# First norm's sums between the first modulation blocks, and tables loaded behind the fourth

## The reference

```python
sh1, sc1, g1, sh2, sc2, g2 = jnp.split(jax.nn.silu(cond) @ p['ada_w'] + p['ada_b'], 6, axis=-1)
hn = rmsnorm(h, p['norm1']) * (1.0 + sc1) + sh1
m, ctx_out = mixer(hn, p['mix'], ctx)
...
def rmsnorm(x, g, eps=NORM_EPS):
    y = xf * lax.rsqrt(jnp.mean(xf * xf, axis=-1, keepdims=True) + eps)
```

## Time and profile before

| | |
|---|---|
| median of 3 runs | 2384.64 us (2384.18 to 2547.99) |
| profiled execution | 2387.17 us |
| its span | 2385.4 us |
| instructions | 41564 |
| TensorE, VectorE, ScalarE, GpSimd busy | 91%, 44%, 27%, 6% |
| mean granted clock of TensorE | 0.935 |

### The profile page before, as it was taken

How to read it: one execution, slowest core, us unless ns; L and a number is a source line. 1 busy time by engine, 2 the same in 40 slices (tenths; PEclk the granted TensorE clock), 3 DMA queues, 4 the chain that set the end, 5 groups by cost and what they waited for, 6 DMA issues and landing times.

```text
span 2385.4 us, 41564 instructions
## 1 busy us (share of the span) xinstructions
PE 2173.5 (91%) x18628; PEld 1811.6 (76%) x18628; DVE 1055.8 (44%) x1875; ACT 653.8 (27%) x1155; POOL 152.8 (6%) x145
## 2 busy tenths in 40 slices
PE   5998787889899999998999868999979899999997
PEld 3554334345799999998999447888855699999997
DVE  0104443331555555324354546867752455555412
ACT  1211332331333233212223433232211233233311
POOL 1000000000000000000000533122100000000000
PEclk8998776899999999998999969999989899999998
DMA  8011442261122221222221000000021122222122
GB/s 306 25 60 57 141 141 71 106 237 45 36 71 77 92 80 49 73 73 65 72 71 45 18 8 3 3 3 4 4 76 36 36 71 71 71 84 71 51 71 69
DMA packets 141409, 163.74 MB, mean 69 GB/s; under 512 B 2368, under 2 KB 106864, under 8 KB 141232
## 3 DMA queue, kind: packets, MB, share of 16 engines
q1 hardware_dynamic: 137872, 148.81, 19.4%
q0 software_dynamic: 3360, 12.28, 1.5%
HBM read 157.32 MB, written 3.75 MB: 68 GB/s over the span
## 4 chain that ended last, share of the span: by engine, by line
PE 82%; DVE 12%; ACT 2%; DMA 1%; issue 1%; ACTq 0%; POOL 0%; DVEq 0%; SPq 0%; POOLq 0%
PE ps L218 76%; PE ps L314 3%; DVE small L907 2%; DMA ring<-in_ada_w 1%; PE ps L829 1%; DVE work L371 1%; ACT work L1322 1%; DVE x_lo_r L384 1%; DVE work L920 1%; DVE work L1797 1%; PE ps L326 1%; DVE work L1361 0%; DVE work L919 0%; DVE stat L322 0%; PE ps L1525 0%
## 5 line engine op out<-in xcount | busy, mean ns | idle before, releaser
L218 PE MATMUL ps<-x_hi_r,w_lo 128*128 128x320 f32 x2080 | 475.9, 310 | 0.0
L218 PE MATMUL ps<-work 64*64 64x64 f32 (+6 forms) x4942 | 384.2, 276 | 36.3 <-DVE work L1862 7.4
L218 PE MATMUL ps<-x_hi_r,w_hi 128*128 128x320 f32 x1664 | 382.0, 311 | 11.3 <-DVE x_lo_r L384 11.3
L218 PE MATMUL ps<-x_lo_r,w_hi 128*128 128x320 f32 x1664 | 382.4, 311 | 8.2 <-DVE g_lo L551 8.2
L218 PEld LDWEIGHTS ps<-work 64*64 64x64 f32 (+4 forms) x4942 | 245.4, 150 | 161.0 <-issue 110.7
L218 PEld LDWEIGHTS ps<-x_hi_r,w_lo 128*128 128x128 f32 x2080 | 348.5, 188 | 0.9
L218 PEld LDWEIGHTS ps<-x_hi_r,w_hi 128*128 128x128 f32 x1664 | 278.9, 188 | 14.8 <-issue 8.6
L218 PEld LDWEIGHTS ps<-x_lo_r,w_hi 128*128 128x128 f32 x1664 | 280.7, 190 | 8.8 <-DVE g_lo L551 8.8
L427 DVE SCALAR_TENSOR_TENSOR work<-ps,par,work 128x511 f32<-128x511 f32 (+1 forms) x188 | 103.5, 550 | 284.2 <-ACT work L527 276.6
L474 DVE TENSOR_TENSOR w_lo<-ring,w_hi 128x1024 fp32r<-128x1024 f32 (+1 forms) x152 | 158.4, 1077 | 100.1 <-ACT w_hi L463 100.1
L463 ACT ACTIVATE w_hi<-ring 128x1024 fp32r<-128x1024 f32 (+1 forms) x152 | 135.6, 937 | 213.3 <-DMA ring<-in_ffn_down 192.5
(11 more groups left out here) (305 smaller groups left out, 2394.7 us busy)
## 6 DMA issues: line engine op xcount, KB each, us to landing
ring<-in_ada_w SPq DMA_DIRECT2D x24, 2048.0 KB, 8.0
ring<-in_ffn_up SPq DMA_DIRECT2D x44, 1024.0 KB, 7.1
ring<-in_ffn_down SPq DMA_DIRECT2D x16, 1408.0 KB, 7.0
ring<-in_l_w_in SPq DMA_DIRECT2D x11, 1024.0 KB, 5.2
ring<-in_l_w_out SPq DMA_DIRECT2D x4, 2048.0 KB, 8.4
ring<-in_l_w_in SPq DMA_DIRECT2D x3, 2048.0 KB, 9.0
h<-in_xT POOLq DMA_DIRECT2D x1, 2560.0 KB, 14.6
out_yT<-work POOLq DMA_DIRECT2D x4, 640.0 KB, 3.9
```

What stands on the lines that cost most here:

```text
L218: return pe.matmul(out, lhsT, rhs, start=first, stop=last)
```

## The change

The squares of the first norm go to the tiles of `hn` instead of the two tiles of `sqb`, so that all eight have a place and no square waits. TensorE sums them directly behind the products of block 0 and ahead of those of block 1. The spread roots go to `sqb`, and `norm_turn` comes between the products of block 1 and the turning of block 0. VectorE inverts and spreads the root ahead of the rows of blocks 1 to 3, which it takes while the roots are being turned (`meanwhile`). The rows of blocks 0 to 3 have banks 0 to 3. ScalarE and VectorE wait for the identity and x alone. `blk` and cosA join the other tables, and GpSimd issues none of these sixteen before all four blocks' products are done.

```diff
-        ada_rows_bank = lambda n: 7 if n >= ADA_FIRST else 6 + n % 2
+        ada_rows_bank = lambda n: 7 if n >= ADA_FIRST else n
...
+        spread_rows = lambda half: stat[:, NT * half:NT * half + NT] if half < 2 else sqb[:, 0:NT]
...
+        square = lambda n, t: hn(t) if n == 0 else tile(sqb, t % 2)
...
-            if t >= 2:
+            if t >= 2 and n > 0:
                 act.wait_ge(sg("norm_sum"), 8 * n + t - 1)
-            act.activation(tile(sqb, t % 2), h(t), ACT.Square).then_inc(sg("norm_sq"), 1)
+            act.activation(square(n, t), h(t), ACT.Square).then_inc(sg("norm_sq"), 1)
...
-            turn_back(pe, 3, 1).then_inc(sg("norm_turned"), 1)
+            turn_back(pe, 3, 1 if n > 0 else 2).then_inc(sg("norm_turned"), 1)
...
-            spread(dve, 0, 1, 1).then_inc(sg("norm_rep"), 1)
+            spread(dve, 0, 1 if n > 0 else 2, 1).then_inc(sg("norm_rep"), 1)
...
-                    pe.wait_ge(sg("m0_loaded"), 16 * 14)
+                    pe.wait_ge(sg("m0_loaded"), 16 * 16)
...
             ada_products(pe, 0, range(KT))
+            for t in range(KT):
+                norm_sum(pe, 0, t)
             for n in range(1, ADA_FIRST):
                 ada_products(pe, n, range(KT))
+                if n == 1:
+                    norm_turn(pe, 0)
                 ada_turn(pe, n - 1)
             ada_turn(pe, ADA_FIRST - 1)
-            for t in range(KT):
-                norm_sum(pe, 0, t)
-            norm_turn(pe, 0)
             mix0_pe(pe)
...
-            act.wait_ge(sg("x_loaded"), 16 * 4)
+            act.wait_ge(sg("x_loaded"), 16 * 2)
...
-            dve.wait_ge(sg("x_loaded"), 16 * 4)
+            dve.wait_ge(sg("x_loaded"), 16 * 2)
...
             ada_take_rows(dve, 0)
-            for n in range(1, ADA_FIRST):
-                ada_take_rows(dve, n)
-                ada_take_cols(dve, n - 1)
-            ada_take_cols(dve, ADA_FIRST - 1)
-            dve.wait_ge(sg("ada_taken"), ADA_FIRST)
-            ada_gain(dve, 0, 0, ch)
-            norm_dve(dve, 0, g_eff(0), ch)
+
+            def other_rows():
+                for n in range(1, ADA_FIRST):
+                    ada_take_rows(dve, n)
+                    ada_take_cols(dve, n - 1)
+                ada_take_cols(dve, ADA_FIRST - 1)
+                dve.wait_ge(sg("ada_taken"), ADA_FIRST)
+                ada_gain(dve, 0, 0, ch)
+            norm_dve(dve, 0, g_eff(0), ch, meanwhile=other_rows)
...
-            pool.dma_start(blk[:, :], cs("blk")).then_inc(sg("x_loaded"), 16)
-            pool.dma_start(cosA, cs("cosA")).then_inc(sg("x_loaded"), 16)
-            for dst, src in ((sinA, cs("sinA")), (cosB, cs("cosB")), (sinB, cs("sinB")), (rotA, cs("rotA")), (rotB, cs("rotB")),
+            pool.wait_ge(sg("ada_rows"), ADA_FIRST)
+            for dst, src in ((blk[:, :], cs("blk")), (cosA, cs("cosA")), (sinA, cs("sinA")), (cosB, cs("cosB")), (sinB, cs("sinB")), (rotA, cs("rotA")), (rotB, cs("rotB")),
```

More of the change, by code:

```diff
@@ L316, in token_sums @@
             return ins
+        spread_rows = lambda half: stat[:, NT * half:NT * half + NT] if half < 2 else sqb[:, 0:NT]
         def spread(dve, i, half, heads):
-            to = stat[:, NT * half:NT * half + NT].rearrange("p (c e x) -> p c e x", c=NCH, e=heads)
+            to = spread_rows(half).rearrange("p (c e x) -> p c e x", c=NCH, e=heads)
             r = root(i, heads).rearrange("p (c e) -> p c e", c=NCH)
@@ L326, in turn_back @@
                 ins = pe.transpose(ps_all[:, 1024 * pair + P * c:1024 * pair + P * c + P],
-                                   stat[:, NT * half + P * c:NT * half + P * c + P], ident[:, :])
+                                   spread_rows(half)[:, P * c:P * c + P], ident[:, :])
             return ins
+        square = lambda n, t: hn(t) if n == 0 else tile(sqb, t % 2)
         def norm_square(act, n, t, base=None):
@@ L355, in norm_sum @@
             pe.wait_ge(sg("norm_sq"), 8 * n + t + 1)
-            ins = token_sums(pe, 3, tile(sqb, t % 2), ones[:, 0:1], t == 0, t == KT - 1)
+            ins = token_sums(pe, 3, square(n, t), ones[:, 0:1], t == 0, t == KT - 1)
             ins.then_inc(sg("norm_sum"), 1)
```

## The result

The changed kernel takes 2382.69 us in the median of 20 runs (2371.09 to 2386.79), the kernel before 2392.99 us in 20 runs (2380.83 to 2547.99). The measured ratio is 0.9936, interval 0.9915 to 0.9956: faster by 0.64%, or 15.3 us of 2393. Repeated against 35 runs of before it was 0.9943 (0.9917 to 0.9969). The two medians themselves differ by 10.3 us, which is at the edge of the interval. So the forecast saving of 15.3 us was met as a ratio, and not by the medians.

A forecast was written before the change was run, and what follows sets the result against it. Bound at the start by arrival of modulation blocks, then by sums nothing overlaps. Sums to 32.7, block 1's products to 36.4, block 3 to 44.2, tail to 52.6: 67.86 - 52.6 = 15.3 saved, median 2369.4 us, range 2361 to 2377.

The forecast's parts named there:

- A shift of that point passes through to the end: First projection's start, 67.86 us before: work behind it is TensorE's own, so 15.3 us saved there shorten the whole.
- The sums' price: Eighty one-column matmuls behind block 0: some 22 at 0.11 us, 58 at 0.213, together 14.8 us, ending at 32.7.
- rival A: First norm's sums: clock stays low throughout, they end at 34.9, start at 54.9, saving 13.0, 2371.7 us; chance 0.18.
- block 3's transfer: DMA ahead of block 3's products: issued at 36.4, takes 7.75 us, ends at 44.2.
- a slower tail: Block 3's products to first projection: forecast unchanged, 6.2 us to the last gain plus 2.2 to first matmul.
- Rival B: First norm's sums run fast, ending at 26.8; first projection at 45, saving 22.9, 2361.8 us; chance 0.09.
- Rival C: First projection's weights arrive last or x lands later: up to 4 us lost, saving 11, 2373.5 us; chance 0.14.
- E: Start of the first projection: an unseen wait keeps it at 67.86, nothing gained, 2384.6 us; chance 0.04.
- the delayed issue: SyncE's ring: block 3 is issued only when block 1 is released, at 36.4 instead of 32.94 us.
- Tables behind the fourth block: GpSimd's sixteen issues from 47.4 on, some 9 us: cost nothing, landed by about 65, first needed at 165.
- the base of the sum: Whole kernel: 15.3 us taken from the before median of 2384.64 us, giving 2369.4.
- Rival D: Stretches behind the start: shifted phases meet more low clock, 60 us of it giving 2399 us; chance 0.03.

The follow-up runs named there:

- the first pair of profiles: One profiled execution each of the unaltered kernel before (2387.17 us, span 2385.4) and the unaltered changed kernel (2386.79 us, span 2385.0).
- the first profile: The changed kernel, unaltered, profiled the first time: 2386.79 us, span 2385.0, first projection at 55.66 us.
- both edits: Changed kernel with first-norm sums that stream the squares and idle products in waits of the norms behind the scan: ratio 0.9858, median 2363.94 us.
- the third profile: The changed kernel, unaltered, profiled once more in one execution: 2373.84 us, span 2372.1, no ratio.

## Why the prediction was right and wrong

*What bounds the kernel.* Right: the sums and the blocks stood alone ahead of the first projection, and moving them moved it. "A shift of that point passes through to the end" held in the first pair of profiles only as far as the second mixer (a lead of 12.2 us at the start, 11.4 there), and as a rule it is too simple: the stretch up to the first up projection varies by up to 9 us between profiles.

*The sums' price.* The term of the sum that failed at the start is "I assume the same course: up about 3 us after 13.9, so near 17, down about 3.4 us later". The clock didn't rise. The eighty took 17.23 us instead of 14.8: rival A, which had 0.18 and a start at 54.9; measured were 55.27 to 55.66 with the changed kernel itself. Of the 3.1 us that the first profile lies behind the forecast of 52.6, 2.4 are the sums; the rest is a start of the sums 0.2 late, block 3's transfer (8.00 instead of 7.75) and a slower tail (8.67 from block 3's products to the first projection instead of 8.4). Rival B, the sums fast, is what streaming the squares brought, and not the change. Rival C did not come: the first projection's wait names ScalarE's shift and not its weights. Nor did E.

The Trainium skill's rule beside rival B ("TensorE: Matmul & The Clock Gate", What's actually happening), that the clock follows how busy TensorE has been, doesn't describe this case as the profile counts busy time: the eighty one-column matmuls filled 17.2 us without a gap and took 0.21 us each to the end, while the clock rose during the streamed sums. Here the measurement decides. With the same section's rule that an idle TensorE falls back to the low level the trace agrees in part: after a wait of 2.75 us, with both edits, block 3's products ran at the low level (3.64 us). But with three idle products in that wait the clock fell as well, if for less long, and the products took 2.25.

*Block 1, block 3 and the delayed issue.* Right in order. Block 3 was issued at 38.9 (forecast 36.4, later by the sums), and root, reciprocal, spread and turning hid behind block 1's products and block 3's transfer. That block 1 would be in at 21.5 was measured with the tables late alone: 21.52. That it is in early had no term of its own in the sum, and has none in the measurement: 0.9945 with the tables early, 0.9943 with them late.

*Tables behind the fourth block.* Right at no cost: GpSimd issued them from 50.8 on, and TensorE's first rotation matmuls came at 169.0 without a wait. The gain's multiplication took 0.17 us beside three issues of GpSimd, as it did before (0.18), and the issues their 0.53. So the 0.5 us that the prediction read from the Trainium skill's rule on the shared ports ("SBUF — State Buffer", SBUF: two separate sides) did not come. That does not speak against the rule: for a VectorE instruction with two SBUF inputs the section limits the lock to GpSimd instructions that read SBUF, a condition that the prediction left out, and no run here shows whether an issue reads any.

*The total.* Here the forecast left its range: the median lies at 2382.69, 13.3 us above 2369.4. Two steps failed. One is the base of the sum, "so the median becomes 2369.4", worked out from a median of three of the kernel before. The other is the width of the range, "executions of one kernel and other chips add a few microseconds". They add up to 18 us with the changed kernel (2368.79 to 2386.79) and 27 with the one before (2380.83 to 2407.36 over all series, its one time of 2547.99 left out). I took the median of three, two of which agreed within 0.5 us, for the kernel's; the median of 20 was 2392.99, 8.35 us higher. My 15.3 us taken from that give 2377.7, just outside the range. The other 5 us are those by which the two medians differ less than 15.3. What the runs showed in place of one time is two: the spans of the changed kernel are 2384.5 and 2385.0 us with the long course of the late stages and 2372.1 with the short one, and more than half of the twenty executions lie in the upper group. The forecast of 2371.9 for the profiled execution is that of an execution with the short course, like the one that it was taken from (measured 2373.84 in the third profile). Rival D named the mechanism, the granted clock in stages that the change doesn't touch, and gave it 0.03, for the wrong reason: it varies without any shift. It looked at 200 to 400 us, where the length varies too, but in the first pair of profiles the loss lay mostly behind 1280 us. As a consequence of the shift it was refuted; as a spread of every execution it was missing from the range.

*The ratio.* It agrees with 15.3 us partly by luck. Of like courses, 13.3 and 14.4 us were saved. The start before varies too (67.86 and 70.94 in two profiles), the start after hardly (55.27 to 55.66 in three, 55.95 with the late stage filled). It would fit that the change also removes the exposed stretch in which the clock could differ, which I had not counted; two profiles of before don't show it.

**Open.** What decides in an execution whether the stages behind 600 us take the short or the long course, and how long the stretch ahead of them is. The two courses were seen with both kernels, and several stages changed together (the channel mixer by 1.1 us, the projections by 1.5, the preparation of the scan by 3.2, the norms behind it by 6.1). Only the last was shown to be the clock by an experiment; for the others it was argued from the mean clock in their rows. Open as well is why filling the norms shortens what stands behind the output projection by 2 us.

## What to carry to other kernels

A share of busy time near 100% doesn't say that TensorE runs at its high clock: here eighty one-column matmuls, which sum over partitions, counted as busy for 17.2 us at the low level. With the ones as weights and the data streaming, the same sums took 9.5 us and left the clock high for what followed. Before a microsecond count from one profile is compared with another, the same program should be profiled twice: here two executions of one kernel differed by 13 us in stages that nobody had touched, as much as the change brought. A median of three can't be taken for the kernel's when its times fall into two groups 10 us apart. Where a chain of small norms leaves TensorE waiting for 1 to 2 us at a time, an idle product in the wait cost nothing in the short course and saved 6 us in the long one; it is worth trying on a kernel that shows a low clock there.

## What the hardware showed that I had not expected

The same stage of the same program has two lengths, 40.2 or 46.3 us, and 281.9 or 286.7, each repeated to 0.2 us. What comes behind can shift with it: filling that stage made the untouched rest 2 us shorter. Sixteen products that directly follow eighty one-column matmuls run at the low rate, 3.64 us; directly after streamed sums they take 1.92. With work on both queues GpSimd's moved 1.21 MB in 275 packets and SyncE's 0.82 MB in 399: the queue with the larger packets moved more. And the inverse of 128 x 640 floats took VectorE 4.15 us, where spreading as many took 0.82.
